# The delta scan without the U and W matrices, with the next head's key product cut into pieces between its steps

## The reference

```python
sol = lax.linalg.triangular_solve(l_mat, rhs, left_side=True, lower=True, unit_diagonal=True)
u, w = sol[..., :dv], sol[..., dv:]        # rhs = [v * beta, k * beta * exp(gcum)]
...
def step(s, xs):
    q_d, k_d, u_c, w_c, a_c, d_c = xs
    v_new = u_c - jnp.einsum('bhcd,bhde->bhce', w_c, s)
    o = jnp.einsum('bhcd,bhde->bhce', q_d, s) + jnp.einsum('bhij,bhje->bhie', a_c, v_new)
    s = s * d_c[..., None, None] + jnp.einsum('bhcd,bhce->bhde', k_d, v_new)
    return s, o
```

## Time and profile before

| | |
|---|---|
| time, three runs | 2116.62 us median (2110.9 to 2116.64) |
| the profiled execution | 2108.15 us, its span 2106.1 us |
| TensorE busy | 2017.4 us, 96% of the span |
| VectorE, ScalarE, GpSimd busy | 55%, 39%, 10% |
| delta heads with a follower (seven) | about 74.8 us each |
| one of them: from the first U product to the end of the scan | 14.9 us |
| from there to the sums of squares of the next head | 18.05 us |

### The profile page before, as it was taken

One profiled execution on the slowest core, in us unless ns is written; L12 is line 12 of the kernel. 1 busy time (PEld: TensorE's weight loads), 2 busy tenths in 40 slices (PEclk: granted clock), 3 DMA queues, 4 the chain that ended last, 5 costly groups with the idle time before them and its releaser, 6 DMA issues.

```text
span 2106.1 us, 31595 instructions
## 1 busy us (share of the span) xinstructions
PE 2017.4 (96%) x11517; PEld 1752.4 (83%) x11517; DVE 1157.1 (55%) x2132; ACT 817.2 (39%) x1315; POOL 209.5 (10%) x211
## 2 busy tenths in 40 slices
PE   7899999999996899999999999999999989999997
PEld 7788888888884679988988898898888858888885
DVE  5877655555446565557666666766533353333335
ACT  2422222211225556565456546536422353222122
POOL 0000000000000120031232133033000000000000
PEclk9999999999998999999999999999999989999998
DMA  7233333333221330011101101100132313223322
GB/s 288 91 120 120 120 120 120 121 127 122 81 83 49 115 115 1 9 38 55 35 30 45 45 20 45 55 18 32 61 100 97 132 50 100 96 94 100 98 92 80
DMA packets 48796, 174.74 MB, mean 83 GB/s; under 512 B 6484, under 2 KB 6612, under 8 KB 48480
## 3 DMA queue, kind: packets, MB, share of 16 engines
q1 hardware_dynamic: 37392, 129.95, 18.4%
q0 software_dynamic: 11344, 43.97, 6.4%
HBM read 167.03 MB, written 4.24 MB: 81 GB/s over the span
## 4 chain that ended last, share of the span: by engine, by line
PE 86%; DVE 7%; ACT 3%; issue 3%; DMA 1%; SPq 0%; POOL 0%; DVEq 0%; ACTq 0%; POOLq 0%
PE ps L1325 79%; PE ps L1329 6%; DMA w_mod<-WMOD 1%; DVE m_part L965 1%; PE ps L1549 1%; DVE d_c L1144 1%; DVE X L873 1%; DVE n_y L865 1%; DVE w_lo L779 1%; DVE d_q L1153 1%; ACT w_hi L398 1%; PE ps L1579 0%; DVE d_r L1157 0%; ACT L644 0%; SPq L265 0%
## 5 line engine op out<-in xcount | busy, mean ns | idle before, releaser
L1325 PE MATMUL ps<-h_hi,w_hi 128*128 128x512 f32 (+1 forms) x1712 | 542.9, 367 | 22.3 <-DVE h_lo L848 17.9
L398 ACT ACTIVATE w_hi<-raw 128x1024 fp32r<-128x1024 f32 x221 | 234.3, 1060 | 821.3 <-PE ps L1325 809.4
L1325 PE MATMUL ps<-h_lo,w_hi 128*128 128x512 f32 (+1 forms) x1712 | 529.1, 359 | 0.0
L1325 PE MATMUL ps<-h_hi,w_lo 128*128 128x512 f32 (+1 forms) x1712 | 528.8, 359 | 0.0
L779 DVE TENSOR_TENSOR w_lo<-raw,w_hi 128x1024 fp32r<-128x1024 f32 x221 | 270.3, 1223 | 416.3 <-ACT w_hi L398 416.1
L1325 PEld LDWEIGHTS ps<-h_hi,w_hi 128*128 128x128 f32 x1712 | 322.2, 190 | 79.7 <-issue 29.9
L1325 PEld LDWEIGHTS ps<-h_lo,w_hi 128*128 128x128 f32 x1712 | 324.4, 190 | 50.8 <-issue 3.4
L1325 PEld LDWEIGHTS ps<-h_hi,w_lo 128*128 128x128 f32 x1712 | 324.0, 189 | 48.9
L1325 PE MATMUL ps<-g_hi,w_hi 128*128 128x512 f32 (+1 forms) x528 | 158.4, 354 | 0.0
L1325 PE MATMUL ps<-g_hi,w_lo 128*128 128x512 f32 (+1 forms) x528 | 157.8, 353 | 0.0
L1325 PE MATMUL ps<-g_lo,w_hi 128*128 128x512 f32 (+1 forms) x528 | 157.8, 353 | 0.0
(11 more groups left out here) (265 smaller groups left out, 2786.9 us busy)
## 6 DMA issues: line engine op xcount, KB each, us to landing
raw<-W SPq DMA_DIRECT2D x221, 512.0 KB, 3.4
w_mod<-WMOD POOLq DMA_DIRECT2D x56, 512.0 KB, 3.7
w_mod<-WMOD SPq DMA_DIRECT2D x4, 2048.0 KB, 22.4
g_row<-g_rows POOLq DMA_DIRECT2D x8, 768.0 KB, 6.0
X<-XT SPq DMA_DIRECT2D x1, 3072.0 KB, 17.9
a_sw<-i_n POOLq DMA_DIRECT2D x40, 64.0 KB, 1.9
x_spill<-X POOLq DMA_DIRECT2D x1, 2048.0 KB, 8.1
X<-x_spill POOLq DMA_DIRECT2D x1, 2048.0 KB, 8.7
```

The lines of the kernel that those rows point to most:

```text
L398: a.activation(w_hi[:, b.pair], raw[:, b.raw], ACT.Copy).then_inc(s("w_hi"), 1)
L1325: return pe.matmul(out, lhsT, rhs, start=start, stop=stop)
```

## The change

The scan no longer uses U and W. In each step, `from_keys` multiplies the keys by the state, VectorE scales by beta e^g and subtracts beta v (`residual`), `solve` applies T, ScalarE copies the new values with the sign turned (`d_vn`, now two buffers), and `to_state` makes the update. The first step applies T to beta v. In a head, `solved` with its 24 products goes, `solve` brings 12 and `from_keys` takes the place of W's 10. ScalarE's 12 scalings of keys, its three copies of U, and VectorE's three copies of W go; ScalarE gets 12 copies, and VectorE's ten subtractions become ten three-operand instructions.

Block 5 is cut up: `fill(n)` issues n of its 48 matmuls. Twelve stand ahead of the scan, 30 between its steps, and 6 behind it. Its weights must be split earlier, so VectorE's `step(b[3])` moves from behind the inversion to behind `masked(6)` in it.

In QKV, `gates_tokens` and `gates_sums` move ahead of the rotation of their round on VectorE; on ScalarE the norm of the last query and its rounding move ahead of the split and the read-out of the two value blocks, and VectorE's last split moves behind the last rotation.

```diff
@@ ScalarE, QKV tail: for j in range(HKV)
                 blk = Blk(B_V, 0, j)
+                if j == 0:
+                    item_rstd(N_ITEM - 1)
+                else:
+                    item_hi(N_ITEM - 1)
                 step(blk)
                 read_out(blk, lambda l, h_: v_raw[j][:, l:h_], segs_all)
                 if j == 0:
-                    item_rstd(N_ITEM - 1)
-                item_hi(N_ITEM - HKV + j)
+                    item_hi(N_ITEM - HKV)
@@ ScalarE, dn_head
...
                 for i in range(18):
...
-                    scaled(i)
-                for gr in range(3):
-                    a.wait_ge(s("uw"), h * 3 + gr + 1)
-                    a.activation(d_q[:, :, 2 * gr:2 * gr + 2].rearrange("p d c n -> p d (c n)"),
-                                 ps[:, UB[gr], :].rearrange("p (d n) -> p d n", d=2), ACT.Copy).then_inc(s("u_c"), 1)
+                    if i < NCH:
+                        scaled(i)
+                for t in range(NCH):
+                    for d in range(2):
+                        a.wait_ge(s("sc_t"), h * 12 + 2 * t + d + 1)
+                        a.activation(d_vn[:, d, t % 2], ps[:, 4 + d, P:2 * P], ACT.Copy, scale=-1.0 if t else 1.0).then_inc(s("sc_n"), 1)
@@ VectorE, QKV: for m in range(N_ITEM + 3)
-                step(Blk(B_QKV, 0, m))
+                if m < N_ITEM + 2:
+                    step(Blk(B_QKV, 0, m))
...
+                if m == 4:
+                    gates_tokens()
+                if m == 5:
+                    gates_sums()
                 if m >= 3:
                     item_rotate(m - 3)
                 if 2 <= m < N_ITEM + 2:
                     item_norm(m - 2)
                 if m >= 3:
                     item_low(m - 3)
-                if m == 4:
-                    gates_tokens()
-                if m == 5:
-                    gates_sums()
                 if m == 6:
                     gates_tables()
+                if m == N_ITEM + 2:
+                    step(Blk(B_QKV, 0, m))
@@ VectorE, dn_head
                 for i in range(18):
                     masked(i)
+                    if i == 6:
+                        step(b[3])
...
-                step(b[3])
...
-                def new_values(t):
+                def residual(t):
                     for d in range(2):
-                        v.wait_ge(s("sc_w"), h * 10 + 2 * (t - 1) + d + 1)
-                        v.tensor_tensor(d_vn[:, d], d_q[:, d, ORDER[d][t]], ps[:, d, 0:P], ALU.subtract).then_inc(s("sc_v"), 1)
+                        c = ORDER[d][t]
+                        v.wait_ge(s("sc_x"), h * 10 + 2 * (t - 1) + d + 1)
+                        v.scalar_tensor_tensor(d_rhs[:, d], ps[:, 4 + d, 0:P], hc[:, G_BEG + 6 * d + c:G_BEG + 6 * d + c + 1],
+                                               d_l[:, d, c], ALU.mult, ALU.subtract).then_inc(s("sc_v"), 1)
...
+                for t in range(NCH):
+                    if t:
+                        residual(t)
                     if t < NCH - 1:
                         new_state(t)
@@ TensorE, dn_head
+                next_key = [(k, i, sg) for k in range(KT) for i in range(3) for sg in segs_all]
+
+                def fill(n):
+                    if final:
+                        return
+                    blk = Blk(B_DN, h, 5)
...
+                    for _ in range(n):
+                        k, i, (l, h_, sg_) = next_key.pop(0)
+                        w, x = ((w_hi, h_hi), (w_hi, h_lo), (w_lo, h_hi))[i]
+                        last = mm(bank(blk, sg_), w[:, blk.pair, k, :], x[:, k, l:h_], k == 0 and i == 0, k == KT - 1 and i == 2)
+                    if not next_key:
+                        last.then_inc(s("gemm_done"), 1)
+
+                def from_keys(t):
                     for d in range(2):
                         c = ORDER[d][t]
+                        pe.wait_ge(s("sc_st"), h * 10 + 2 * (t - 1) + d + 1)
+                        mm(ps[:, 4 + d, 0:P], d_c[:, 1, off[c]:off[c] + P], d_st[:, d]).then_inc(s("sc_x"), 1)
+
+                def solve(t):
                     for d in range(2):
+                        c = ORDER[d][t]
                         if t:
                             pe.wait_ge(s("sc_v"), h * 10 + 2 * (t - 1) + d + 1)
+                        mm(ps[:, 4 + d, P:2 * P], d_r[:, d, c], d_rhs[:, d] if t else d_l[:, d, c]).then_inc(s("sc_t"), 1)
+
+                def to_state(t):
                     for d in range(2):
+                        pe.wait_ge(s("sc_n"), h * 12 + 2 * t + d + 1)
+                        mm(ps[:, 6 + d, 0:P], d_kd[:, d, ORDER[d][t]], d_vn[:, d, t % 2]).then_inc(s("sc_s"), 1)
...
+                fill(12)
                 pe.wait_ge(s("d_vb"), h * 2 + 2)
                 pe.wait_ge(s("d_am"), h * 2 + 2)
+                pe.wait_ge(s("sv_r"), h * 3 + 2)
+                solve(0)
+                fill(3)
                 pe.wait_ge(s("d_kd"), h * 2 + 2)
                 pe.wait_ge(s("sv_r"), h * 3 + 3)
-                from_values(0)
-                solved(2)
...
+                to_state(0)
+                fill(3)
+                for t in range(1, NCH):
+                    from_keys(t)
+                    if t > NC_CTX:
+                        out_values(t - 1)
+                    else:
+                        fill(3)
+                    solve(t)
+                    if t == NC_CTX:
+                        pe.wait_ge(s("d_qd"), h * 2 + 2)
+                    if t >= NC_CTX:
+                        out_state(t)
+                    else:
+                        fill(3)
+                    if t < NCH - 1:
+                        to_state(t)
+                    fill(3)
+                out_values(NCH - 1)
+                fill(len(next_key))
```

More of the change, by code:

```diff
@@ L184, in build @@
         d_st = at("d_st", 202.25, [2, P])
[L185 removed]
+        d_rhs = at("d_rhs", 203.25, [2, P])
         d_o = at("d_o", 204.25, [SEQ])
@@ L1639, in dn_head @@
                 grow(17)
-                pe.wait_ge(s("d_vb"), h * 2 + 2)
-                pe.wait_ge(s("d_kb"), h * 2 + 2)
-                pe.wait_ge(s("d_am"), h * 2 + 2)
-                def solved(gr):
-                    pe.wait_ge(s("sv_r"), h * 3 + gr + 1)
-                    for d in range(2):
-                        for k in range(2):
-                            c, o_ = 2 * gr + k, P * (2 * d + k)
-                            mm(ps[:, UB[gr], o_:o_ + P], d_r[:, d, c], d_l[:, d, c])
-                    for d in range(2):
-                        for k in range(2):
-                            c, o_ = 2 * gr + k, P * (2 * d + k)
-                            last = mm(ps[:, WB[gr], o_:o_ + P], d_t[:, d, c], d_r[:, d, c])
-                    last.then_inc(s("uw"), 1)
@@ L1655, in from_state @@
-                def from_state(t):
-                    for d in range(2):
-                        pe.wait_ge(s("sc_st"), h * 10 + 2 * (t - 1) + d + 1)
-                        mm(ps[:, d, 0:P], d_wc[:, d, ORDER[d][t]], d_st[:, d]).then_inc(s("sc_w"), 1)
+                next_key = [(k, i, sg) for k in range(KT) for i in range(3) for sg in segs_all]
[3 more added lines that the diff above has]
+                    blk = Blk(B_DN, h, 5)
+                    if len(next_key) == 6 * KT:
+                        pe.wait_ge(s("w_split"), blk.n + 1)
+                        pe.wait_ge(psum_read[blk.pair], blk.turn + 1)
+                    for _ in range(n):
[4 more added lines that the diff above has]
+                        last.then_inc(s("gemm_done"), 1)
@@ L1659, in from_state @@
+                def from_keys(t):
                     for d in range(2):
                         c = ORDER[d][t]
-                        if c >= NC_CTX:
-                            mm(ps[:, 2 + d, P * (c - NC_CTX):P * (c - NC_CTX) + P], d_st[:, d], d_qd[:, d, c - NC_CTX], True, False)
-                def from_values(t):
-                    vn = [d_vn[:, d] if t else d_q[:, d, ORDER[d][t]] for d in range(2)]
+                        pe.wait_ge(s("sc_st"), h * 10 + 2 * (t - 1) + d + 1)
+                        mm(ps[:, 4 + d, 0:P], d_c[:, 1, off[c]:off[c] + P], d_st[:, d]).then_inc(s("sc_x"), 1)
@@ new lines, in out_state, with out_values @@
+                def out_state(t):
+                    for d in range(2):
+                        o_ = P * (ORDER[d][t] - NC_CTX)
+                        mm(ps[:, 2 + d, o_:o_ + P], d_st[:, d], d_qd[:, d, ORDER[d][t] - NC_CTX], True, False)
+                def out_values(t):
+                    for d in range(2):
+                        o_ = P * (ORDER[d][t] - NC_CTX)
+                        pe.wait_ge(s("sc_n"), h * 12 + 2 * t + d + 1)
+                        mm(ps[:, 2 + d, o_:o_ + P], d_vn[:, d, t % 2], d_at[:, d, ORDER[d][t] - NC_CTX], False, True)\
+                            .then_inc(s("sc_o"), 1)
@@ L1685, in dn_head @@
-                from_values(1)
-                pe.wait_ge(s("w_c"), h * 3 + 3)
-                pe.wait_ge(s("u_c"), h * 3 + 3)
```

(8 more changed lines are left out.)

45 lines of the change are left out of this document (9 added, 36 removed).

## The result

The changed kernel takes 2152.1 us, the median of four runs (2142.39 to 2153.69), against 2113.76 for the kernel before (four runs, 2109.7 to 2116.64). The ratio is 1.0177, with a 95% interval of [1.0145, 1.0208]: slower, inside the range, 2.6 us over the predicted 2149.5. The profiled execution took 2153.69 us, its span is 2152.0.

The account below looks back on a forecast made before the run. TensorE's queue was taken as the bound except behind the scan, where an 18.05 us VectorE and ScalarE chain binds. 23.1 + 0.7 + 12.9 - 0.3 - 3.5 = +32.9 us on the median 2116.62 gave 2149.5, range 2122 to 2168.

Parts of the forecast that it names:

- The bound behind the scan: From scan end to the sums of squares: a VectorE and ScalarE chain, staying 18.05 us whatever TensorE work is removed.
- the rival in which TensorE bounds it: Behind the scan: removing block 5 pieces shortens the stretch, 4.05 us gained a head, time 2085, faster; chance 0.10.
- The condition given for it: Behind the scan: TensorE bounds only if the VectorE and ScalarE chain takes less than 14.7 us.
- One of the signs: Profile after, scan end to sums of squares: still 18 us, with TensorE idle for over 6 us of it.
- The scan: Scan in seven heads: 18.24 us against 14.93, +3.3 a head, +23.1 in all (bounds +21.8 to +33).
- the loop of six handoffs: One scan step: dependent handoffs between engines total 2.53 us, just covered by TensorE's 2.75 us; 0.2 us added for waits.
- The last head: Last head's scan, without block 5: bare loop of 14.6 us against 14.93, -0.3 (bounds -1 to +2).
- The clock: Behind the scan: idle time lowers TensorE's clock, block 2 ends 0.35 us too late; 0.1 a head taken, +0.7.
- The rival by which the block behind the squares would run at half clock: After the 2.65 us gap before the squares: 3.0 us lost a head, time 2170; clock or loop much worse, chance 0.13.
- The split: VectorE's w_lo in the inversion, eight heads: held up by GpSimd's mask, next product 1.61 us late, +12.9 (bounds 0, +16).
- QKV: QKV stage: gates release TensorE 3.95 us sooner, some clock loss returned, reordered tail costs 1.0; together -3.5 (bounds -8, -2).
- The 0.6 us that the clock was to give back: QKV, behind the earlier gates: 0.6 of the 3.0 us lost at half clock is recovered (bounds 0 and 3.0).

Follow-up runs that it names:

- the lighter fill: Changed kernel with the weight split behind the sixth mask and only 26 of block 5's 48 matmuls inside the scan, 22 behind: 2114.95 us, ratio 1.0016.
- the kernel with the early split: As the lighter fill, but VectorE splits the next block 2's weights inside the scan, behind the fifth step's residual: 2107.54 us, ratio 0.9987.
- the run with the early decays: As the kernel with the early split, plus the next head's decay differences and minima (d_q, d_t) moved into the scan: 2088.07 us, ratio 0.9879.
- the full fill: The fastest kernel with block 5 placed in the scan as thickly as in the changed kernel (12 ahead, 3 per gap): 2097.34 us, ratio 0.9949.
- the fastest kernel: As the run with the early decays, with the order of the last QKV items put back: 2081.5 us; repeated, 2081.26 us, ratio 0.9878.

## Why the prediction was right

*The bound behind the scan.* Right. The stretch stayed at 18.05 us with 42 pieces less in it (18.05 predicted), and the rival in which TensorE bounds it fell in three ways: by the kernel after, by block 5 put back (18.07), and by the lighter fill (no 40 us). The condition given for it, that the chain be under about 14.7 us, was met only once the chain was shortened, and then the kernel did become faster. One of the signs was not met: TensorE was to be idle for over 6 us of the stretch, and it was for 4.65, since block 2 took 2.6 us more at the lower clock.

*The scan.* +3.3 a head predicted, +3.4 measured (19.92 against 16.52 from the first `d_r` to the end). The sum was right, one of its parts was not: the loop of six handoffs takes 2.79 us, not 2.53 + 0.2, so it is the loop and not only TensorE's work (2.75) that sets a late step. Both were so near that the total hid it. The bare loop shows it, in the run with block 5 behind the scan (17.00 us against 16.52) and in the last head.

*The last head.* -0.3 predicted for its scan, +0.56 measured: 17.11 us against 16.55 from the first `d_r` to the last output product, within the bounds, and the term with the wrong sign. But this head grew by 3.4 us. 1.5 of that is the held-up split, which has its own term; 1.2 is the clock, at the start of the inversion. Behind the same two waits, of 1.10 and 1.03 us, the first 16 matmuls with `d_w` and `d_s`, with those between them, took 6.14 us instead of 4.92. The windows, in the kernel after and then before, columns as above:

```profile
1488.72:1492.00 3.28, 3.28 (x15) 3.28 (x16) 1.05 (x2) 1.34 (x4) 2.77 (x2) 0.50 0.00 0
```

```profile
1444.86:1448.20 3.34, 3.30 (x26) 3.11 (x27) 1.73 (x3) 1.69 (x6) 3.18 (x3) 1.00 0.00 0
```

No term had this, and little ties it to the change: of the eleven profiles with the solve in the scan the clock fell in this part of the last head in six, with and without block 5 in the scan, and not in the other five; with U and W it did in neither of two.

*The clock.* +0.7 predicted. The clock fell as foreseen: block 2 began at 1063.50 and ended at 1074.48, 10.98 us instead of 8.4, at 0.81 over the stretch. It ended just when the squares were ready, so in this head it cost nothing, and at most 0.1 us in the others. The rival by which the block behind the squares would run at half clock did not occur in the kernel after, and did, at 1.7 us a head, in the kernel with the early split: the idle time there stood directly ahead of the products on the path.

*The split.* 1.61 a head predicted, 1.56 by the start of the eighth mask's product, 1.55 by the run with the split one mask earlier. The wait of the eighth product is 1.40 us instead of the 1.6 given as a sign. The Trainium skill, "SBUF — State Buffer", section "Who interferes with whom", has it that such a pair contends and that the order of issue decides which of the two blocks. In this place the trace agrees (GpSimd 0.12 us ahead, the split held up), as it does for the split of the second pair in the earlier trace rows; for L1144 of the first pair, which started 0.30 us ahead of GpSimd and was held, it does not.

*QKV.* -3.5 predicted, -2.5 measured. The gates came 3.95 us sooner, as worked out, and the tail cost 1.1 (1.0 predicted). The 0.6 us that the clock was to give back did not come: the block took 23.12 us against 22.78.

*Sum.* Eight splits, seven scans and the last head come to +38.9 against the predicted +36.4, and 1.2 of the 2.5 between is the clock in the last head. QKV is -2.5 against -3.5. The -1.4 behind the heads was not foreseen. It goes with the clock again: over 30 us around the norm ahead of the second FFN stage it was 0.77 before (1705 to 1735) and 0.83 after (1750 to 1780), and in the thirteen profiles the time from the last output product of the heads to the end is 621.2 to 621.9 us with about 10 us at half clock there, and 622.0 to 622.6 with about 14. In all 35.0 against 32.9. The terms carry the result, but that the total is met to 2.6 us is in part luck: the base of the forecast, the median 2116.62, and the median after, 2152.1, were both, by their values, of runs at the FFN's slower rate.

## What to carry to other kernels

Before moving work from one stretch to another, find what sets the length of both: work that is taken from a stretch bound by a chain of other engines comes back as idle time, and what is filled in beyond the gaps of the other is paid in full. A dependent loop with handoffs between three engines is a good place for independent work, but only up to its idle time, here three pieces a step; the better use of the room was on the engines of the chain. A long operation with two inputs in SBUF has to be placed by what GpSimd does at that moment: one mask earlier it was not held at all, and two masks later it cost 0.3 us instead of 1.55. And a clock that falls in one execution and not in the next moves a head by more than a microsecond, so read the granted clock before a difference of that size is given a cause.

## What the runs showed of the hardware

- The same 3336 matmuls of the first FFN stage took 569.7 to 571.0 us in some executions and 580.2 to 581.4 in others, TensorE busy throughout and the granted clock at 1.00 in both, as one window of before and one of after show. What decides it stays open.

```profile
62.64:633.34 570.70, 570.70 (x3337) 505.21 (x3338) 340.13 (x831) 132.92 (x177) 28.49 (x54) 1.00 0.34 112
```

```profile
62.81:644.17 581.36, 581.36 (x3337) 506.49 (x3338) 340.19 (x831) 132.80 (x177) 28.51 (x54) 1.00 0.33 110
```

- Behind the same wait of 2.48 us in QKV the granted clock over the next 6 us was 0.50 in the kernel after (23.12 us to the end of the block), 0.72 in the run with the early decays and in that with the full fill, and 1.00 in the fastest kernel (19.98 us):

```profile
712.51:732.49 19.98, 19.98 (x86) 15.52 (x87) 14.07 (x29) 10.37 (x20) 5.47 (x12) 1.00 0.38 109
```

- Behind the same two waits of 1.10 and 1.03 us in the last head, with TensorE busy for 2.24 of 4.48 us (1484.24 to 1488.72) in the kernel after and for 2.24 of 4.56 (1440.30 to 1444.86) before, the granted clock was 0.50 over the next 3.28 us in the one and 1.00 in the other. What decides it stays open.

- The split of weights took 1.22 us alone, 2.77 behind GpSimd's 1.81 us mask, and 1.54 at most behind the ninth mask; the operation of GpSimd that came next was prolonged too, from 1.46 to 2.45 us.
